# A recurrent branch in 64-row products, two chunks per set, with state steps woven in

## The reference, cut to what matters

```
sk = einsum('bhij,bhj->bhi', state, kk_t)
state = state * w_t - sk[..., None] * (kk_t * a_t)[:, :, None, :] + v_t[..., None] * k_t[:, :, None, :]
y = einsum('bhij,bhj->bhi', state, r_t)
```

## Time and profile before

| | us |
|---|---|
| three timed runs | 2580.59, 2590.91, 2586.76 (median 2586.76) |
| profiled execution | 2589.36 |
| its span, first to last instruction | 2587.5 |
| PE / DVE / ACT busy | 2289.5 / 1553.6 / 1022.5 |
| mean granted TensorE clock | 0.949 of full speed |

### The profile page before, as it was taken

One profiled execution on the slowest core, in us unless ns is written; L12 is line 12 of the kernel. 1 busy time (PEld: TensorE's weight loads), 2 busy tenths in 40 slices (PEclk: granted clock), 3 DMA queues, 4 the chain that ended last, 5 costly groups with the idle time before them and its releaser, 6 DMA issues.

```text
span 2587.5 us, 42572 instructions
## 1 busy us (share of the span) xinstructions
PE 2289.5 (88%) x14624; PEld 2039.8 (79%) x14632; DVE 1553.6 (60%) x3005; ACT 1022.5 (40%) x1634; POOL 19.3 (1%) x27
## 2 busy tenths in 40 slices
PE   7998888999799977999767777998788999999998
PEld 6997876899699856998656654786776799999997
DVE  4556776655555445556544345688976666666665
ACT  4334544533433445334421134322542344444443
POOL 0000000000000000000000000000000000000000
PEclk9998988999899998999889878999999999999999
DMA  5554333455555433554300011443235666666664
GB/s 189 186 186 155 131 136 101 161 178 186 196 195 190 139 93 114 188 186 144 116 1 0 0 50 49 130 146 122 106 138 177 213 210 212 201 203 186 187 186 137
DMA packets 106663, 376.86 MB, mean 146 GB/s; under 512 B 11552, under 2 KB 17456, under 8 KB 105840
## 3 DMA queue, kind: packets, MB, share of 16 engines
q1 hardware_dynamic: 102528, 354.88, 41.9%
q0 software_dynamic: 4080, 21.28, 2.6%
HBM read 362.42 MB, written 13.69 MB: 145 GB/s over the span
## 4 chain that ended last, share of the span: by engine, by line
PE 76%; DVE 9%; ACT 5%; DMA 4%; issue 4%; DVEq 2%; ACTq 1%; SPq 0%
PE bank L340 57%; PE bank L366 6%; PE bank L1298 3%; DVE w_lo L301 2%; DMA ring<-in_expert_v 2%; PE bank L2001 1%; DMA ring<-in_ssm_in 1%; ACT w_hi L296 1%; DVE arena L2202 1%; DMA ring<-in_expert_u 1%; PE bank L1342 1%; PE bank L531 1%; PE bank L1278 1%; DVE arena L1523 1%; PE bank L768 1%
## 5 line engine op out<-in xcount | busy, mean ns | idle before, releaser
L301 DVE TENSOR_TENSOR w_lo<-ring,w_hi 128x1024 fp32r<-128x1024 f32 x581 | 701.5, 1223 | 465.4 <-ACT w_hi L296 463.8
L296 ACT ACTIVATE w_hi<-ring 128x1024 fp32r<-128x1024 f32 x581 | 604.2, 1056 | 704.3 <-PE bank L340 540.2
L340 PE MATMUL bank<-u_hi,w_hi 128*128 128x256 f32 x2568 | 733.8, 286 | 21.0 <-DVE w_lo L301 12.5
L340 PE MATMUL bank<-u_lo,w_hi 128*128 128x256 f32 x2568 | 730.6, 284 | 0.0
L340 PE MATMUL bank<-u_hi,w_lo 128*128 128x256 f32 x2568 | 730.2, 284 | 0.0
L340 PEld LDWEIGHTS bank<-u_hi,w_hi 128*128 128x128 f32 x2568 | 496.6, 193 | 32.0 <-issue 11.6
L340 PEld LDWEIGHTS bank<-u_lo,w_hi 128*128 128x128 f32 x2568 | 496.6, 193 | 7.6 <-issue 0.5
L340 PEld LDWEIGHTS bank<-u_hi,w_lo 128*128 128x128 f32 x2568 | 496.1, 193 | 0.0
L340 PE MATMUL bank<-w_hi,x_hi 128*128 128x512 f32 x992 | 396.2, 399 | 22.0 <-DVE w_lo L301 14.5
L340 PE MATMUL bank<-w_lo,x_hi 128*128 128x512 f32 x992 | 393.1, 396 | 0.0
L340 PE MATMUL bank<-w_hi,x_lo 128*128 128x512 f32 x992 | 390.8, 394 | 0.0
(11 more groups left out here) (321 smaller groups left out, 1975.5 us busy)
## 6 DMA issues: line engine op xcount, KB each, us to landing
ring<-in_w SPq DMA_DIRECT2D x264, 512.0 KB, 3.6
ring<-in_expert_u SPq DMA_DIRECT2D x128, 512.0 KB, 3.7
ring<-in_expert_v SPq DMA_DIRECT2D x128, 512.0 KB, 4.2
ring<-in_ssm_in SPq DMA_DIRECT2D x40, 512.0 KB, 4.4
gate_dram<-con SPq DMA_DIRECT2D x16, 576.0 KB, 2.9
arena<-gate_dram POOLq DMA_DIRECT2D x9, 1024.0 KB, 8.6
ring<-in_ssm_out SPq DMA_DIRECT2D x16, 512.0 KB, 3.4
ring<-in_w_o SPq DMA_DIRECT2D x16, 512.0 KB, 4.1
```

The costliest lines, as they stand in the source:

```text
L296: act.activation(w_hi[slot][:, :], ring[slot][:, :], ACT.Copy).then_inc(hi_made[slot], 1)
L301: dve.tensor_tensor(w_lo[slot][:, :], ring[slot][:, :], w_hi[slot][:, :].bitcast(F32), ALU.subtract).then_inc(freed[slot], 1)
L340: mm = pe.matmul(out, left[a], right[b], start=start and n == 0, stop=stop and n == 2, skip_group_check=True)
```

## The change

The block-diagonal matrices go. A head matrix is held as 64 columns: partitions carry the two heads, and the 512 columns of a tensor carry four pairs times two chunks. All products of the stage become 64x64 (grams 64x192), one for each half, through a helper `tile64`. The four chunks form two sets of two. One inversion runs for both chunks of a set, with the same eight levels; a bank of a level is then 16 products and 32 records in place of 4 and 8. The loops are unrolled. PE's list of set 1's inversion has the state work of chunks 0 and 1 and the g of chunk 2 between its levels, and that of chunks 2 and 3 stands among latents 0 to 3. Latents 4 and 5 follow, and then the sums of y. ACT copies y out of PSUM in place of DVE. Many tensors move, some are kept twice (one for each set), constants shrink to 64 columns, and the loads of latents 4 and 5 are issued ahead of uv and the positions.

```diff
-        rights = area(26504, 4, 3, CH)
...
-        diag_alpha, diag_beta, diag_kappa, diag_v = (area(at, 4, P) for at in (24968, 0, 512, 1024))
...
-        (U, UL, A, AL, A2, AL2, A4) = (area(5200 + 512 * n, 4, P) for n in range(7))
...
+        rights = [pairs(at, 3, CH) for at in (0, 24712)]
+        beta, kappa = pairs(21640, CH), pairs(22152, CH)
+        U, UL, A, AL, A2, AL2, A4 = (pairs(5200 + 512 * n, CH) for n in range(7))
+        AL4, NL = pairs(17544, CH), pairs(18056, CH)
+        N = [pairs(at, CH) for at in (4608, 26760)]
+        of_kappa = [pairs(at, 3, CH) for at in (1536, 11912)]
+        of_beta = [pairs(at, 2, CH) for at in (3072, 13448)]
+        v_st = [pairs(at, CH) for at in (4096, 26248)]
+        z_st = [area(at, 4, CH) for at in (27272, 15496)]
...
+        LATENT = (bank[0], bank[1], bank[2], bank[3], bank[5], bank[6])
...
-            with pe.Fori(0, RC) as c:
...
+            def tile64(b, at, *products):
+                for a in halves:
+                    for n, (left, right) in enumerate(products):
+                        width = right.shape[-1]
+                        mm = pe.matmul(bank[b][a, at:at + width], left[a, :], right[a, :],
+                                       start=(n == 0), stop=(n == len(products) - 1))
+                return mm
+            eight = [(p, cc) for p in range(4) for cc in range(2)]
+            def level(*products):
+                for b, left, right in products:
+                    for j, (p, cc) in enumerate(eight):
+                        mm = tile64(b, j * CH, (left[:, p, cc, :], right[:, p, cc, :]))
+                mm.then_inc(S("inv_done"), 1)
...
+            def state_g(c):
+                G, cc = c // 2, c % 2
+                pe.wait_ge(S("lk_ready"), c + 1)
+                pe.wait_ge(S("rows_ready"), G + 1)
+                pe.wait_ge(S("z_ready"), c + 1)
                 for p in range(4):
+                    mm = tile64(7, 256 + p * CH, (rights[G][:, p, cc, 0:CH], z_st[c % 2][:, p, :]),
+                                (of_kappa[G][:, p, cc, 0:CH], v_st[G][:, p, cc, :]))
+                mm.then_inc(S("g_done"), 1)
+            def state_s(c):
+                G, cc = c // 2, c % 2
+                pe.wait_ge(S("inv_sum"), 6 * G + 6)
+                pe.wait_ge(S("g_ready"), c + 1)
+                if c:
+                    pe.wait_ge(S("y_kept"), c)
                 for p in range(4):
+                    mm = tile64(4, p * CH, (N[G][:, p, cc, :], g_st[:, p, :]))
+                mm.then_inc(S("s_done"), 1)
+            def state_step(c):
+                G, cc = c // 2, c % 2
+                pe.wait_ge(S("s_ready"), c + 1)
                 for p in range(4):
+                    mm = tile64(7, p * CH, (of_kappa[G][:, p, cc, 2 * CH:3 * CH], v_st[G][:, p, cc, :]),
+                                (of_beta[G][:, p, cc, CH:2 * CH], s_neg[:, p, :]))
+                mm.then_inc(S("step_done"), 1)
+                for p in range(4):
+                    mm = tile64(4, 256 + p * CH, (z_st[c % 2][:, p, :], rights[G][:, p, cc, CH:2 * CH]),
+                                (v_st[G][:, p, cc, :], of_kappa[G][:, p, cc, CH:2 * CH]),
+                                (s_neg[:, p, :], of_beta[G][:, p, cc, 0:CH]))
+                mm.then_inc(S("step_done"), 1)
...
+            def invert(G, between):
+                NG = N[G]
+                pe.wait_ge(S("inv_sum"), 6 * G + 1)
+                pe.wait_ge(S("rows_ready"), G + 1)
+                level((5, AL, A), (6, A, AL))
+                between(1)
+                pe.wait_ge(S("inv_copied"), 5 * G + 1)
+                pe.wait_ge(S("gram_read"), G + 1)
+                level((2, AL2, A2), (3, A2, AL2), (0, AL2, NG), (1, A2, NL))
+                between(2)
+                pe.wait_ge(S("inv_copied"), 5 * G + 2)
+                pe.wait_ge(S("inv_sum"), 6 * G + 2)
+                level((5, AL4, A4), (6, A4, AL4), (0, AL4, NG), (1, A4, NL))
+                gram_kappa(G, 0)
+                between(3)
+                pe.wait_ge(S("inv_copied"), 5 * G + 3)
+                pe.wait_ge(S("inv_sum"), 6 * G + 3)
+                level((0, AL2, NG), (1, A2, NL))
+                pe.wait_ge(S("lk_ready"), 2 * G + 1)
+                gram_kappa(G, 1)
+                between(4)
+                pe.wait_ge(S("inv_sum"), 6 * G + 4)
+                level((5, AL, NG), (6, A, NL))
+                between(5)
+                pe.wait_ge(S("inv_copied"), 5 * G + 4)
+                pe.wait_ge(S("lk_ready"), 2 * G + 2)
+                level((2, NL, A2), (3, NG, A4))
+                between(6)
+                pe.wait_ge(S("inv_sum"), 6 * G + 5)
+                level((5, AL, NG))
+                between(7)
+                pe.wait_ge(S("inv_copied"), 5 * G + 5)
+                level((6, NL, A2))
+            def ahead_of_second(k):
+                if k == 7:
+                    gram_beta(1)
+                    state_g(0)
+            def first_states(k):
+                if k == 1:
+                    state_step(0)
+                if k == 2:
+                    state_g(1)
+                if k == 3:
+                    state_s(1)
+                if k == 4:
+                    state_step(1)
+                if k == 6:
+                    state_g(2)
+            gram_beta(0)
+            gram_alpha(0)
+            invert(0, ahead_of_second)
+            pe.wait_ge(S("inv_sum"), 6)
+            gram_alpha(1)
+            state_s(0)
+            invert(1, first_states)
+            def latent(n):
+                pe.wait_ge(S("inv_sum"), 12)
+                project_split(pe, LATENT[n][:, 0:T], n % 4, "mla", 0, n // 4)
+            state_s(2)
+            latent(0)
+            state_step(2)
+            latent(1)
+            state_g(3)
+            latent(2)
+            state_s(3)
+            latent(3)
+            state_step(3)
+            latent(4)
+            latent(5)
+            pe.wait_ge(S("lat_out"), 4)
...
+            def keep_y(c):
+                act.wait_ge(S("step_done"), 2 * c + 2)
+                act.activation(y_rw[:, :, c * CH:(c + 1) * CH], bank[4][:, 256:512].rearrange("p (a b) -> p a b", a=4),
+                               ACT.Copy).then_inc(S("y_kept"), 1)
...
+            def prepare(G):
+                now = slice(2 * G * CH, 2 * (G + 1) * CH)
+                def chunks(t):
+                    return t[:, :, now].rearrange("p q (c x) -> p q c x", c=2)
+                dve.tensor_copy(all_of(third(rights[G], 2)), over(C("eye"), 8))
+                dve.tensor_tensor(third(rights[G], 0), chunks(p_prev), chunks(kk), ALU.mult)
+                dve.tensor_tensor(third(rights[G], 1), chunks(p_now), chunks(R_), ALU.mult)
+                dve.tensor_tensor(beta, chunks(p_inv), chunks(kk_a), ALU.mult).then_inc(S("chunk_ready"), 1)
+                dve.tensor_tensor(kappa, chunks(p_inv), chunks(K_), ALU.mult).then_inc(S("chunk_ready"), 1)
...
+            grams(1)
+            state_s(0)
+            rest_of_grams(1)
+            state_z(0)
+            add(1, 2, ALU.add, (N[1], 0), (NL, 1)).then_inc(S("inv_sum"), 1)
+            state_g(1)
+            add(1, 3, ALU.add, (N[1], 0), (NL, 1)).then_inc(S("inv_sum"), 1)
+            state_s(1)
+            mask_level(32)
+            kappas(1, 0)
+            add(1, 4, ALU.add, (N[1], 0), (NL, 1)).then_inc(S("inv_sum"), 1)
+            state_z(1)
+            kappas(1, 1)
             for n in range(2):
                 make_lo(dve, n, "mla", 0)
+            add(1, 6, ALU.subtract, (N[1], 2), (NL, 3))
+            mask_level(64).then_inc(S("inv_sum"), 1)
+            state_g(2)
+            add(1, 8, ALU.subtract, (N[1], 6)).then_inc(S("inv_sum"), 1)
...
-            sp.wait_ge(S("y_rw_ready"), 1)
...
+            for n in range(4, 6):
+                load(sp, n % 4, io["mla_in"][n, :, :], "mla", 0, n // 4)
+            sp.wait_ge(S("z_ready"), 4)
```

More of the change, by code:

```diff
@@ L1292, in rwkv_tensor @@
[L1292 to L1304, removed]
@@ L1405, in rwkv_scalar, with copies @@
-            for n in range(4):
-                make_hi(act, n, "mla", 0)
+            def copies(G, done, *moves):
+                act.wait_ge(S("inv_done"), 8 * G + done)
+                for b, dst in moves:
+                    ins = act.activation(row(dst), bank[b][:, :], ACT.Copy)
+                ins.then_inc(S("inv_copied"), 1)
+            def keep_y(c):
+                act.wait_ge(S("step_done"), 2 * c + 2)
+                act.activation(y_rw[:, :, c * CH:(c + 1) * CH], bank[4][:, 256:512].rearrange("p (a b) -> p a b", a=4),
+                               ACT.Copy).then_inc(S("y_kept"), 1)
@@ new lines, in rwkv_scalar @@
+            for G in range(2):
+                act.wait_ge(S("rows_done"), G + 1)
+                act.activation(row(v_st[G]), bank[6][:, :], ACT.Copy).then_inc(S("rows_ready"), 1)
+                copies(G, 1, (5, A2), (6, AL2))
+                if G:
+                    keep_y(0)
+                copies(G, 2, (2, A4), (3, AL4))
```

(39 more changed lines are left out.)

270 lines of the change are left out of this document (95 added, 175 removed).

## The result

The changed kernel takes 2504.28 us (median of 4, 2499.17 to 2508.38) against 2588.84 (4 runs): a ratio of 0.9678, 95% interval 0.9655 to 0.97, so 84.6 us less. 2512 had been forecast, with 2494 to 2552 as the range. The profiled execution took 2499.17 us, span 2497.2, mean clock 0.95.

A forecast was written before the change was run, and what follows sets the result against it. The kernel was taken to be bound by a chain of waits around PE, no engine full. Savings of 79.1 + 8.1 = 87 us gave 2502; a clock loss of 11 made 2513, stated as 2512, range 2494 to 2552.

The forecast's parts named there:

- Entry: Start of the stage: DVE prepares both chunks, cold beta gram, alpha gram, masks and subtractions; 12.2 us.
- Set 0: Eight inversion levels of the first two chunks, with kappa grams and the next set's beta gram between; 30.9 us.
- Between the sets: Alpha gram 1.2 us and four DVE operations 2.6 us between the two inversions; 3.8 us.
- Set 1: Second inversion with the state work of chunks 0 and 1 between its levels; 32.4 us.
- Tail: State work of chunks 2 and 3 (6.5 us) among four latents (11.5 us); 18.0 us.
- Latents 4 and 5: Two latents standing in PE's queue ahead of the sums of y; 5.8 us.
- After: From the sums of y to the latent sums: 9.8 + 9.7 + 3.3 = 22.8 us, 8.1 less than before.
- The clock: Over the stage, a granted clock of 0.85 as in the old turns was to cost 11 us.
- Rival A: Clock stays at half through the stage, or records cannot be fed faster: 63 us more, 2565; full or part 0.27.
- Rival B: Fetching the unrolled code: 8 more instruction packets, 10 us unhidden, 2523; counted inside the forecast's own range.
- Rival C: The halves do not run side by side and the clock stays low: 181 us more, 2683; chance 0.03.

The follow-up runs named there:

- e1: The changed kernel run once more, unedited, as yardstick for other runs; 2502.89 us, ratio 0.9674 to the kernel before.
- e12: Changed kernel with angles in DVE's wait, sums of y ahead of the last latents, and set 1's 32-wide masks ahead of chunk 1's s; 2485.95 us, 0.9608.
- e5: Changed kernel with latents 0 to 3 taken out of the tail, so all six latents follow the states of chunks 2 and 3; 2497.30 us, 0.9657.
- e7: Changed kernel with the last two latents moved in PE's queue behind the first and the second sums of y; 2494.98 us, 0.9643.
- e6: Changed kernel with DVE's eleven angle operations moved from behind its work on y into its wait for ACT's root; 2492.53 us, 0.963.
- e3: Kernel before with only the 64-column layout and 64x64 products, one chunk per turn, loop written out, latents behind the branch; 2525.00 us, 0.9763.
- e2: Changed kernel with all upper-half 64x64 records of a level ahead of all lower-half ones, instead of alternating; 2556.05 us, 0.9874.
- e8: Changed kernel with both edits: angles moved into DVE's wait and sums of y ahead of the last latents; 2489.49 us, 0.962.

## Why the prediction was right, and where it was off

**Entry, 12.2: 10.1.** The beta gram was forecast cold at 5.1 and the alpha gram at 1.95 with the handover. The two took 5.1 together (1304.04 to 1309.14): the clock rose inside the beta gram (to 1.00 near 1307), which took 4.0. In e1 the clock rose later, the beta gram took 5.2 and the two 6.6. So the price of the cold gram was right, and that the clock rose so early was luck.

**Set 0, 30.9: 33.0.** Levels with ACT's or DVE's pair: 3.26, 5.43, 5.42, then 6.72 for the fourth and fifth (6.8), 4.07. The last two with the beta gram between took 8.06, not 6.3. The clock fell there, after a wait of 1.99 for DVE; in e1, where the same wait stands and the clock stayed up, the same PE piece took 5.68 in place of 7.34:

```profile
1336.78 7.32 PE L1289 MATMUL bank<-arena 64*64 64x64 f32 x128 [1.99 <-DVE arena L1637]
```

```profile
1337.80:1341.20 3.40, 3.40 (x30) 2.65 (x28) 0.00 (x0) 0.60 (x1) 0.00 (x0) 0.54 0.02 5
```

**Between the sets, 3.8: 3.95. Set 1, 32.4: 33.0.** PE waited 0.78 for the second kappa gram (1.0 forecast), 8.36 after level 3 began (8.3). e12 shows that DVE's order makes that wait.

**Tail, 18.0: 20.0.** This term was too small. I had priced latents and steps by their records alone, 2.88 and 2.32, and they took 3.06 and 2.64. The last record of one shape and the first of the next start 0.15 to 0.21 apart instead of 0.03 or 0.12, and a step's groups of two and three products run at 0.031. By e5 a latent among steps and a step among latents each cost some 0.15 more. "TensorEngine Tiling" in the Trainium skill (Key Properties) says that changing the tile mode drains the engine; the trace agrees, with 0.15 to 0.21 us between these starts.

**Latents 4 and 5, 5.8: 5.94.** e7 shows that they were indeed in the way: 6.2 us back when the sums of y pass them.

**After, 22.8: 22.2**, and its links were the ones named: e6 takes DVE's part out and the stage loses 8.8.

**The clock, 11 us: the step that was mis-sized.** I had carried over the 0.85 of the turns. The granted clock from the preparation to the sums of y was 0.97, and the only slow stretch between the entry and the sums of y cost 1.7 (7.34 - 5.68). From the preparation to the latent sums the forecast was 103.1 + 22.8 + 11 = 136.9 us and the trace has 128.2. Of the 8.7 too much, 9.3 are the clock, 2.1 the entry and 0.6 the stretch behind the sums of y; against them stand the 2.0 left out in the tail and 1.3 in small pieces. That is the forecast's 8. The terms without the clock gave 2502, in the profiled execution's time, which came to 2499.2; this nearness is partly luck, since they are 2.3 us short in the stage and 5.3 us of the two spans' difference lie outside it. Rival A falls: 0.97, not under 0.75, and 128 records in 3.95 us, 0.03 each, with no limit of supply. What decides between the two levels is not shown: e3 had both for the same bursts, and e2 both for the same kind of level.

**Rival B.** 13 packets more in the instruction queue (8 forecast), and no wait put down to them shows in the stage. Its 10 us were not paid there.

**Rival C.** Halves written one product at a time into one bank ran at 0.029. The 0.107 that it feared exists, but only where the halves do not take turns (e2): even that order left the kernel at 0.987 of the time before. Why it was not slower than before, as C would have it, no run takes apart. "TensorEngine Tiling" (Gotcha 1: PSUM Pressure) in the Trainium skill says that different row tiles cannot access one PSUM bank at the same time and leaves it to the software to keep them apart. The prediction took this for a wait of each half for the other; no level of the changed kernel shows one (0.029 a record, both halves in one bank).

## What to carry to other kernels

When a product fills only half of the rows, do not pad: emit the two halves as neighbours in turn, and check the start spacing in the trace (0.029 here, 0.0585 if the order is wrong). After such a change read the chain once more from its end. The two places that it named, a DVE operation block behind a wait with room in it and latents queued ahead of sums that were ready, gave 14.5 us of stage more for a few moved lines (e8). Take the stage's time from the trace beside the run's time: effects of 5 us were clear in the one and lost, or of the other sign, in the other.

## What the runs showed of the hardware that was not expected

- PE's busy share alone did not set the granted clock. One half of the rows at a time, 100% busy, was granted 0.50 in one level of e2 (13.5 us) and 1.00 in another (7.1 us). Both halves in turn, 67% busy with waits between, had 1.00 in e3's second turn, and in its first fell to 0.50 for 13.65 us.
- Records of the two halves overlap in some measure out of strict alternation: 0.029 a record in turn, 0.038 in runs of four products, 0.0585 in runs of 8 to 32 products, at full clock. In turn, the starts come in pairs: 0.007 us within a pair and 0.052 to the next one.
- ACT's first sine behind the root has a table load of 1.28 us ahead of it (e6, L1869, ACT_TABLE_LOAD). In the changed kernel that lay beside DVE's work on y; with the angles moved it is on the chain, and it is the next thing to move.
